# A fused transformer kernel in which GpSimd subtracts the second part of every fourth weight tile, in two stages

## The reference

```python
h = rmsnorm(x, g_pre) * (1.0 + scale) + shift
proj = h @ w_in                       # 1024 x 8864
ya = differential_attention(...) @ da_w_o
yb = softmax_attention(...) @ mla_w_o
yc = (sc_b * causal_dwconv(sc_c * sc_u, sc_conv)) @ sc_w_o
u  = causal_dwconv(cf_a * sigmoid(cf_g), cf_conv)     # 31 taps
yd = silu(layernorm(u + cf_conv_b)) @ cf_w_o
merged = g0 * ya + g1 * yb + g2 * yc + g3 * yd
x = x + gate1 * rmsnorm(merged @ w_mix_out, g_post)
```

## Time and profile before

| | us |
|---|---|
| median of 3 runs | 3227.44 |
| lowest and highest of them | 3226.8, 3230.92 |
| the profiled execution | 3228.79 |
| its span in the profile | 3227.0 |
| PE busy in the span | 3145.3 (97%) |
| DVE busy | 2482.0 (77%) |
| ACT busy | 1773.0 (55%) |
| POOL busy | 3.0 (0%) |

### The profile page before, as it was taken

One profiled execution on the slowest core, in us unless ns is written; L12 is line 12 of the kernel. 1 busy time (PEld: TensorE's weight loads), 2 busy tenths in 40 slices (PEclk: granted clock), 3 DMA queues, 4 the chain that ended last, 5 costly groups with the idle time before them and its releaser, 6 DMA issues.

```text
span 3227.0 us, 64473 instructions
## 1 busy us (share of the span) xinstructions
PE 3145.3 (97%) x27118; PEld 3064.1 (95%) x27118; DVE 2482.0 (77%) x3822; ACT 1773.0 (55%) x2721; POOL 3.0 (0%) x6
## 2 busy tenths in 40 slices
PE   6999999999999999989999999999999999998999
PEld 6999999988999999989999989999979999997999
DVE  8998899988887766896676677667667667679766
ACT  4556555566564544675554555455456455467544
POOL 0000000000000000000000000000000000000000
PEclk9999999999999999999999999999999999999999
DMA  7456578445756555536555535555544555553553
GB/s 296 153 190 227 193 270 309 168 132 164 248 172 234 164 189 190 164 118 196 188 183 189 189 128 190 188 178 192 188 130 154 189 185 185 188 184 110 178 187 129
DMA packets 164353, 597.94 MB, mean 185 GB/s; under 512 B 18240, under 2 KB 18272, under 8 KB 163936
## 3 DMA queue, kind: packets, MB, share of 16 engines
q1 hardware_dynamic: 164064, 593.81, 55.4%
HBM read 592.69 MB, written 1.05 MB: 184 GB/s over the span
## 4 chain that ended last, share of the span: by engine, by line
PE 82%; DVE 12%; ACT 3%; issue 2%; DMA 1%; SPq 0%; DVEq 0%; ACTq 0%
PE ps L497 26%; PE ps L499 25%; PE ps L498 25%; DVE wlo L456 4%; DVE fa L1854 1%; PE ps L504 1%; ACT whi L444 1%; PE ps L510 1%; PE ps L505 1%; DMA land<-w_ada 0%; ACT h L2034 0%; DMA land<-w_in 0%; PE ps L1432 0%; DVE land L663 0%; PE ps L799 0%
## 5 line engine op out<-in xcount | busy, mean ns | idle before, releaser
L497 PE MATMUL ps<-h,whi 128*128 128x256 f32 x5136 | 1445.8, 282 | 6.6 <-DVE wlo L456 4.0
L499 PE MATMUL ps<-h,wlo 128*128 128x256 f32 x5184 | 1449.9, 280 | 0.0
L498 PE MATMUL ps<-h,whi 128*128 128x256 f32 x5136 | 1436.8, 280 | 0.0
L456 DVE TENSOR_TENSOR wlo<-land,whi 128x1024 fp32r<-128x1024 f32 (+1 forms) x1026 | 1213.8, 1216 | 195.4 <-ACT whi L444 194.0
L444 ACT ACTIVATE whi<-land 128x1024 fp32r<-128x1024 f32 (+1 forms) x1026 | 1029.1, 1045 | 215.2 <-PE ps L499 185.6
L497 PEld LDWEIGHTS ps<-h,whi 128*128 128x128 f32 x5136 | 967.7, 188 | 11.2 <-DVE wlo L456 6.9
L499 PEld LDWEIGHTS ps<-h,wlo 128*128 128x128 f32 x5184 | 976.4, 188 | 0.0
L498 PEld LDWEIGHTS ps<-h,whi 128*128 128x128 f32 x5136 | 967.7, 188 | 0.8
L499 PE MATMUL ps<-y,wlo 128*128 128x256 f32 x1472 | 411.1, 279 | 0.0
L498 PE MATMUL ps<-y,whi 128*128 128x256 f32 x1472 | 411.1, 279 | 0.0
L497 PE MATMUL ps<-y,whi 128*128 128x256 f32 x1472 | 411.1, 279 | 0.0
(11 more groups left out here) (483 smaller groups left out, 3232.7 us busy)
## 6 DMA issues: line engine op xcount, KB each, us to landing
land<-w_gu SPq DMA_DIRECT2D x352, 512.0 KB, 3.5
land<-w_dn SPq DMA_DIRECT2D x176, 512.0 KB, 3.5
land<-w_in SPq DMA_DIRECT2D x136, 512.0 KB, 3.6
land<-w_ada SPq DMA_DIRECT2D x96, 512.0 KB, 4.5
land<-w_up SPq DMA_DIRECT2D x88, 512.0 KB, 4.0
land<-hg_in SPq DMA_DIRECT2D x64, 512.0 KB, 3.5
land<-w_down SPq DMA_DIRECT2D x44, 512.0 KB, 4.3
land<-ple_gate SPq DMA_DIRECT2D x32, 512.0 KB, 3.5
```

The source lines that it names most:

```text
L456: dve.tensor_tensor(w.lo, g.slot(n), w.hi.bitcast(F32), ALU.subtract).then_inc(*D_("w_lo", n))
L497: pe.matmul(out, w.hi, x.hi, start=first, stop=False, skip_group_check=skip)
L498: pe.matmul(out, w.hi, x.lo, start=False, stop=False, skip_group_check=skip)
L499: return pe.matmul(out, w.lo, x.hi, start=False, stop=last, skip_group_check=skip)
```

## The change

In tiles 0 to 92 and 166 to 258, every tile whose number leaves 3 when divided by 4 has its second part written by GpSimd instead of VectorE: 23 tiles in each of the two stages, 46 in all. GpSimd's program now begins with these 46 subtractions, each behind a wait for its tile's `w_hi`. TensorE waits for a new semaphore, `pool_low`, at these tiles. VectorE's walk over the tiles is as before but leaves them out; the lists of steps, the DMAs, ScalarE's work and the rings are unchanged.

```diff
@@ -451,10 +451,26 @@
         i = g.ahead["dve"]
         n = g.split[i]
         g.ahead["dve"] = i + 1
-        w = g.weights(n)
-        dve.wait_ge(*W("w_hi", n))
-        dve.tensor_tensor(w.lo, g.slot(n), w.hi.bitcast(F32), ALU.subtract).then_inc(*D_("w_lo", n))
+        if not by_pool(g, n):
+            w = g.weights(n)
+            dve.wait_ge(*W("w_hi", n))
+            dve.tensor_tensor(w.lo, g.slot(n), w.hi.bitcast(F32), ALU.subtract).then_inc(*D_("w_lo", n))
         modulation_vector(g, dve, n)
+
+
+def by_pool(g, n):
+
+    first = [g.split[0], g.index["w_down", 21] + 1]
+    return any(f <= n <= g.index["w_mix_out", 8 * lay] for lay, f in enumerate(first)) and g.part[n] % 4 == 3
+
+
+def low_gpsimd(g, pool):
+    D_, W = g.m.done, g.m.when
+    for n in g.split:
+        if by_pool(g, n):
+            w = g.weights(n)
+            pool.wait_ge(*W("w_hi", n))
+            pool.tensor_tensor(w.lo, g.slot(n), w.hi.bitcast(F32), ALU.subtract).then_inc(*D_("pool_low", n))
 
@@ -489,7 +505,7 @@
 def take_tensor(g, pe, name, i):
     n = g.index[name, i]
-    pe.wait_ge(*g.m.when("w_lo", n))
+    pe.wait_ge(*g.m.when("pool_low" if by_pool(g, n) else "w_lo", n))
     return n
@@ -3656,6 +3672,7 @@
 def gpsimd_program(g, pool):
+    low_gpsimd(g, pool)
     for n in (0, 3):
         hgrn_gpsimd(g, pool, f"mx{n}")
```

## The result

The changed kernel takes 3258.51 us (median of 4 runs, 3256.29 to 3261.78) against 3227.59 us (median of 4 runs): ratio 1.0093, 95% interval 1.0081 to 1.0104. It is slower by about 30 us. The forecast was 3245 us and slower.

What follows compares the result with a forecast made beforehand. VectorE was taken as the chain from 42 to 217 us and in part of 600 to 755 us. Terms 9.8 + 1 + 7.7 - 1 = 17.5 us on 3228.8 gave 3246.3, stated as 3245 us, range 3217 to 3263.

Steps and rivals of the forecast that it cites:

- tile 171: At a stage start in `m1`, GpSimd would end about 1 us later than VectorE did, TensorE waiting: +1 us.
- The price of one tile: On VectorE, each moved tile costs 1.84 us held and saves 1.14 us: +0.70 us.
- The share of 0.8: From 42 to 217 us, VectorE has two-input SBUF operations in hand near 80% of the time: 0.8 x 2.3 us held.
- The number of tiles that count: Tiles priced at +0.70 us: 14 from 42 to 217 us, 11 from 600 to 755 us; 9 after each, nothing.
- to 217 us: From 42 to 217 us in `m0`, VectorE being the chain: 14 tiles at 0.70, 9.8 us slower.
- 217 to 345: In `m0` with TensorE full: 9 tiles' 6.3 us fit in VectorE's 18.5 us free, so nothing.
- 600 to 755: In `m1`: 11 tiles at 0.70, 7.7 us, less 1 us for VectorE's lead over TensorE.
- 755 to the end: From 755 to 880 us in `m1`: 6.3 us against 18.2 us free on VectorE, so nothing.
- worse place: In VectorE's short softmax and norm chains, a hold falls worse than the removed subtraction, which sat in gaps; not in the sum.
- No contention: Rival: VectorE loses nothing to GpSimd and has 52 us less to do; 9 us faster, 3219 us; chance 0.22.
- VectorE first: Rival: GpSimd starts only in VectorE's gaps, TensorE stands at late fourth tiles; about +27 us, 3255; chance 0.12.
- Sharing by the column: Rival: both engines share the SBUF path column by column, VectorE losing about 1.1 us each; 3228, no change; chance 0.14.

Runs made afterwards that it cites:

- first 28 tiles: Changed kernel with GpSimd given only tiles 3 to 55 and 167 to 219, 28 of the 46: 3253.44 us, ratio 1.0080.
- the small program: Stand-alone program replacing the whole computation: 16 VectorE subtractions of 256 columns take 5.46 us alone, 11.89 us beside three GpSimd subtractions of 1024 columns.
- the run with the old place: Changed kernel, with each GpSimd subtraction also waiting for VectorE's second part of the tile before it: 3254.56 us, ratio 1.0078.
- The run with only the last tiles: Changed kernel with GpSimd given only tiles 59 to 91 and 223 to 255, 18 of the 46: 3234.12 us, ratio 1.0019.
- eighths: Changed kernel with each GpSimd subtraction cut into eight pieces of an eighth of the columns: 3238.36 us, ratio 1.0028.

## Why the prediction was right, and where its sizes were off

**Direction and mechanism: right.** VectorE is the chain in `m0`, it is held by GpSimd's reads, the hold is in its records and not on a semaphore, and TensorE stands longer on lines behind VectorE. GpSimd's duration was taken as 2.3 us; it is 2.31 us back to back (6.93 / 3), 2.35 the shortest in the kernel, 2.64 with waits. PSUM operations are not held. GpSimd's tiles are in time; the one exception that was forecast, tile 171, isn't waited for either. The rest were steps of the forecast.

**The price of one tile: right.** Forecast 1.84 us held less 1.14 saved, +0.70. Measured 1.79 held less 1.06 saved, +0.73 (33.3 us over 46 tiles, from the pages). That it fits to 0.03 us is in part luck. The share of 0.8 was reasoned as a share of time, but a collision takes what is left of a whole instruction: in the stretches where VectorE is densest, held time is 1.86 us (first 28 tiles: (2504.5 - 2482.0) / 28 + 1.06), which is 0.87 of the 2.14 us that the small program shows, where the forecast had 0.8 of 2.3.

**The number of tiles that count: the step that failed.** 46 x 0.73 = 33 us is the whole growth of VectorE's busy time, and the span grew by 31. The sum had only 25 tiles' worth and took 1 us off. It also had no term for the clock, though the forecast named it as a thing to look at: 7.4 of the 31 us are slower matmuls. That 33 and 31 lie so close is therefore no proof of a simple rule. Term by term, against the lag table:

| stretch | forecast | measured |
|---|---|---|
| to 217 us | 9.8 | 16.0 |
| 217 to 345 | 0 | 5.3 |
| 345 to 600 | 1 | 1.2 |
| 600 to 755 | 6.7 | 8.2 |
| 755 to the end | 0 | 0.4 |
| together | 17.5 | 31.1 |

- *To 217 us.* VectorE's busy time grew by 11.1 us in the stretch (176.45 - 165.38), near the forecast 9.8. On top came the 2.3 us of lag at 45 us, before the stretch. Some 1.8 us of it are tile 3, whose hold fell into the first normalized chunks, where TensorE waits for each (one chunk's record at 36.03 us is 2.28 us long, its neighbours 0.47); the text named that place but priced it as any other. And VectorE itself stood 3 us longer (12.6 us idle for 9.6), in its exchanges with ScalarE. These two are the "worse place" that stood outside the sum; the run with the old place lowers the start's 2.3 to 0.5, but is later by as much elsewhere.
- *217 to 345 us, "nothing".* Wrong. 18.5 us of free time on VectorE did not cover 6.3 us of work, because free time is not where the work is late. One result of VectorE, the second part of a branch's activations, came only 0.1 us before TensorE took it; the hold of one subtraction 10 us ahead of it became 2.1 us of standstill, and with the lower clock behind it 3.4 us of lag. TensorE was idle for 3.7 us in the stretch where it had 0.2. The run with only the last tiles shows it apart: 4 us there.
- *755 to 880 us, "nothing".* Right, at 0.4 us, with the same arithmetic: here TensorE hardly stood (0.2 us idle of 125). The arithmetic doesn't tell the two apart, and neither do the leads of the tiles, which before the change were ready 1.7 to 12.0 us ahead (median 6.3, tiles 59 to 91) and 2.2 to 12.9 us (7.8, tiles 223 to 255). At the one place that the trace of the last tiles shows, it was the lead of activations that VectorE makes, which the busy times by stretch don't hold; the leads of all such results in the two stretches were not compared.

**Rivals.** No contention (3219) is out: 2.14 us for one subtraction, where 1.14 was the point at which it turned. Its prize was also too large: 5 us measured for 9 taken. VectorE first (3255) came nearest in time (3258.5 measured) and is wrong in mechanism: GpSimd gets its turn, mostly after one VectorE instruction at the most and in two cases of 46 after some 2.2 us, VectorE then waits for it, and no tile is late. Sharing by the column (3228) is out by the records of 2.56 us.

**The asymmetry.** Taking 49 us off VectorE gave 5 us, adding 33 us cost 31, adding 99 us cost 95, and adding nothing on balance (eighths) still cost 9.6. The forecast treated relief and hold as one net sum per tile, which is right for busy time; but it put 18 of the 46 tiles at zero, as if lateness too could be absorbed, and left out what the clock adds to a standstill.

## What to carry to other kernels

Before moving a two-input operation from VectorE to GpSimd, price it as nearly GpSimd's whole duration on VectorE, not as zero, unless VectorE works on PSUM there; here that is up to 2.1 us held (1.8 on average) for 1.1 us saved. Where two engines are nearly level, work added to the one that is behind can arrive nearly whole while work taken off is hardly seen, so measure with the work left out before looking for another engine to do it. And free time in a stretch hides a delay only if it lies between the delayed instruction and the one that waits for it: read how long before its reader each result is done, activations as well as weight tiles, and not the busy share.

## What the runs showed of the hardware beyond that

- A VectorE product with a constant on two columns of SBUF, 155 ns by itself, lasted up to 2.33 us when it met a GpSimd subtraction; in the kernel the softmax's such step went from 169 to 609 ns on average up to 230 us. Size does not protect.
- Three ScalarE copies of 1024 columns beside GpSimd subtractions took 2.95 us together, records of 1.04 us, no longer than in the kernels (1.05 us each): ScalarE wasn't held here.
- A GpSimd subtraction of n columns took 0.41, 0.68 and 2.31 us for n = 128, 256 and 1024 back to back: about 0.14 us and 2.1 ns a column.
- The mean granted clock fell from 0.98 to 0.96 in the stretch of `m0` where TensorE stands still more, and its busy time there grew by 3.6 us (171.83 for 168.23): a standstill of 2.1 us cost 3.4 to 3.6 us where the clock was at 1.2 GHz behind it.
